# First chunk behind a full-width norm taken as two summands, and made whole last

## The reference

```python
for layer in range(DEPTH):                                  # DEPTH = 2
    h = rms_norm(r, norm_mix_pre[layer])
    proj = h @ w_in[layer]                                  # latents first, then q, k, v, gates
    ...                                                     # MLA and differential attention, gates
    mix = (sigmoid(g_a) * out_a + sigmoid(g_b) * out_b) @ w_out[layer]
    r = r + rms_norm(mix, norm_mix_post[layer])
    h = rms_norm(r, norm_ffn_pre[layer])
    gu = h @ w_gate_up[layer]
    ff = (silu(gu[..., :D_FF]) * gu[..., D_FF:]) @ w_down[layer]
    r = r + rms_norm(ff, norm_ffn_post[layer])
```

## Time and profile before

| What | Value |
| --- | --- |
| Median of 3 runs | 794.01 us |
| Profiled execution | 794.08 us |
| Its span | 792.3 us |
| PE busy | 785.0 us, 99% of the span |
| DVE busy | 572.3 us, 72% |
| ACT busy | 451.7 us, 57% |
| POOL busy | 138.6 us, 17% |
| TensorE clock granted | 0.999 of full, mean |
| HBM traffic | 169 GB/s over the span |

### The profile page before, as it was taken

How to read it: one execution, slowest core, us unless ns; L and a number is a source line. 1 busy time by engine, 2 the same in 40 slices (tenths; PEclk the granted TensorE clock), 3 DMA queues, 4 the chain that set the end, 5 groups by cost and what they waited for, 6 DMA issues and landing times.

```text
span 792.3 us, 16792 instructions
## 1 busy us (share of the span) xinstructions
PE 785.0 (99%) x6268; PEld 762.2 (96%) x6268; DVE 572.3 (72%) x996; ACT 451.7 (57%) x766; POOL 138.6 (17%) x150
## 2 busy tenths in 40 slices
PE   9999999999999999999999999999999999999997
PEld 9999899999999999999999999999999999999885
DVE  6899787696787666766668987967866977676432
ACT  6657665675475454455557467656755755454331
POOL 0312000233321111101123302001433211111000
PEclk9999999999999999999999999999999999999999
DMA  9767433355166565355654674334552776667971
GB/s 334 255 225 241 131 109 107 107 187 160 55 206 218 161 176 172 115 166 170 198 173 134 192 241 153 107 108 132 187 167 73 227 215 178 195 175 193 276 135 54
DMA packets 55531, 134.87 MB, mean 170 GB/s; under 512 B 20896, under 2 KB 21536, under 8 KB 55344
## 3 DMA queue, kind: packets, MB, share of 16 engines
q1 hardware_dynamic: 38608, 131.43, 52.9%
q10 hardware_dynamic: 16864, 2.62, 2.0%
HBM read 131.93 MB, written 2.10 MB: 169 GB/s over the span
## 4 chain that ended last, share of the span: by engine, by line
PE 97%; DVE 1%; ACT 1%; issue 0%; DVEq 0%
PE bank L1330 24%; PE bank L1332 24%; PE bank L1331 24%; PE bank L1364 4%; PE bank L1748 3%; PE bank L1749 3%; PE bank L1747 3%; PE bank L1355 2%; PE bank L1602 2%; PE bank L1574 2%; PE bank L1621 1%; PE bank L1449 1%; PE bank L1423 1%; PE bank L1576 1%; PE bank L1380 1%; PE bank L1391 1%
## 5 line engine op out<-in xcount | busy, mean ns | idle before, releaser
L883 DVE TENSOR_TENSOR w_lo<-w_raw,w_hi 128x1024 fp32r<-128x1024 f32 x246 | 330.9, 1348 | 37.4 <-ACT w_hi L438 34.5
L1330 PE MATMUL bank<-h_hi,w_hi 128*128 128x272 f32 (+1 forms) x1200 | 346.0, 288 | 0.0
L1332 PE MATMUL bank<-h_hi,w_lo 128*128 128x272 f32 (+1 forms) x1200 | 342.8, 286 | 0.0
L1331 PE MATMUL bank<-h_lo,w_hi 128*128 128x272 f32 (+1 forms) x1200 | 341.9, 285 | 0.0
L438 ACT ACTIVATE w_hi<-w_raw 128x1024 fp32r<-128x1024 f32 x246 | 258.5, 1054 | 122.1 <-PE bank L1332 57.0
L1330 PEld LDWEIGHTS bank<-h_hi,w_hi 128*128 128x128 f32 x1200 | 226.2, 188 | 0.7
L1332 PEld LDWEIGHTS bank<-h_hi,w_lo 128*128 128x128 f32 x1200 | 226.2, 188 | 0.0
L1331 PEld LDWEIGHTS bank<-h_lo,w_hi 128*128 128x128 f32 x1200 | 226.0, 188 | 0.0
L848 POOL TENSOR_TENSOR pbuf<-sbuf,ubuf 128x272 f32<-128x272 f32 (+1 forms) x44 | 38.5, 874 | 205.6 <-DVE ubuf L1260 204.0
L779 POOL TENSOR_TENSOR acc<-acc,sq 128x272 f32<-128x272 f32 (+1 forms) x45 | 47.3, 1052 | 137.2 <-ACT sq L451 137.0
L1260 DVE TENSOR_TENSOR ubuf<-bank,rstd_h 128x272 f32<-128x272 f32 (+1 forms) x44 | 18.9, 430 | 44.9 <-PE bank L1332 44.9
(11 more groups left out here) (238 smaller groups left out, 1229.2 us busy)
## 6 DMA issues: line engine op xcount, KB each, us to landing
w_raw<-weights SPq DMA_DIRECT2D x216, 512.0 KB, 3.9
w_raw<-weights SPq DMA_DIRECT2D x16, 384.0 KB, 3.2
w_raw<-weights SPq DMA_DIRECT2D x16, 320.0 KB, 2.9
w_first<-first_weights SPq DMA_DIRECT2D x2, 512.0 KB, 7.5
x_tok<-x_rows SPq DMA_DIRECT2D x1, 1024.0 KB, 11.0
turn<-y ACTq DMA_DIRECT2D x4, 256.0 KB, 7.1
r_tok<-turn ACTq DMA_DIRECT2D x8, 128.0 KB, 6.3
out_tokens<-o_tok SPq DMA_DIRECT2D x4, 256.0 KB, 2.0
```

What stands on the lines that cost most here:

```text
L883: dve.tensor_tensor(w_lo[:, n % RING, :], w_raw[:, n % RAW, :], w_hi[:, n % RING, :].bitcast(f32), ALU.subtract).then_inc(lo_ready, 1)
L1330: pe.matmul(dst, wh, hi, start=first, stop=False)
L1331: pe.matmul(dst, wh, lo, start=False, stop=False)
L1332: return pe.matmul(dst, wl, hi, start=False, stop=last)
```

## The change

Chunk 0 of the stream behind a post-norm is `old + new`: the old residual, known early, and the normed part's product. Both times the gain are split into high and low parts of their own. ACT makes `old_hi` behind the sixth output tile, DVE `old_lo` behind the seventh. The PE multiplies the first four tiles' weights of chunk 0 with the old part inside `post_norm`: two tiles ahead of the transposes in place of 10 dummy matmuls, two tiles behind them, with 8 dummies in place of 28. Behind the transposes DVE makes `new` first, ACT rounds it to `new_hi`, and the first tiles take it as their chunk 0. DVE and ACT then make chunks 1 to 7, and last the whole chunk 0 (`CHUNK_ORDER`). The fifth tile takes the chunks in that order; it has the norm sums ahead of its fifth chunk, and the spread (FFN only) ahead of its last. Its last chunk waits for all low parts. In `first_tiles` the bank waits of the boundaries move into `old_part`, one for each tile.

```diff
+CHUNK_ORDER = [1, 2, 3, 4, 5, 6, 7, 0]
...
+            def old_high(b):
+                t0 = boundary_from(b)
+                act.activation(old_hi[:, t0:], r[:, 0, t0:], ACT.Copy, scale=first_gain(b)).then_inc(old_hi_ready, 1)
...
-                for c in range(KC):
-                    act.wait_ge(r_ready, KC * (b - 1) + c + 1)
+                act.wait_ge(new_ready, b)
+                act.activation(new_hi[:, t0:], new[:, t0:], ACT.Copy, scale=first_gain(b)).then_inc(new_hi_ready, 1)
+                for c in CHUNK_ORDER:
+                    if c == 0:
+                        act.wait_ge(r_first_ready, b)
+                    else:
+                        act.wait_ge(r_ready, (KC - 1) * (b - 1) + c)
+                    high(c)
+                    square(K, CHUNK_ORDER.index(c), r[:, c, t0:], t0)
...
                     square_tile(K0 + POST_MIX, TL("out") + m, m)
+                    if m == 5:
+                        old_high(2 * l + 1)
...
+                dve.scalar_tensor_tensor(out=new[:, t0:], in0=y[:, 0, t0:], scalar=gain[:, lp, gp:gp + 1],
+                                         in1=ps[7][:, 64 + t0:64 + TOK], op0=ALU.mult, op1=ALU.mult).then_inc(new_ready, 1)
...
-                product(0)
-                add(0)
                 product(1)
                 add(1)
-                for c in range(2, KC):
+                product(2)
+                new_low()
+                add(2)
+                for c in range(3, KC):
                     product(c)
                     lo_part(b, c - 2, *nxt(b), t0)
                     add(c)
                 lo_part(b, KC - 2, *nxt(b), t0)
+                dve.wait_ge(new_ready, b)
+                dve.tensor_tensor(r[:, 0, t0:], r[:, 0, t0:], new[:, t0:], ALU.add).then_inc(r_first_ready, 1)
                 lo_part(b, KC - 1, *nxt(b), t0)
+                lo_part(b, 0, *nxt(b), t0)
...
                     to_y(K0 + POST_MIX, TL("out") + m, m)
+                    if m == 6:
+                        old_low(2 * l + 1)
...
+            def fifth_tile(b, t, n, src, t0, inside):
+                bank_free(t)
+                for at, k in enumerate(CHUNK_ORDER):
+                    if at in inside:
+                        inside[at]()
+                    if k == 0:
+                        pe.wait_ge(h_lo, KC * (b + 1))
+                    mm = block(t, n, k * P, P, *src[k], t0, at == 0, at == KC - 1)
+                mm.then_inc(pe_done, 1)
...
+            def old_part(b, tiles):
+                pe.wait_ge(old_lo_ready, b)
+                slot_ready(tiles[-1][1])
+                for t, n, _, t0 in tiles:
+                    bank_free(t)
+                    dst = ps[bank_of(t)][:, t0:TOK]
+                    pe.matmul(dst, w_hi[:, n % RING, 0:P], old_hi[:, t0:], start=True, stop=False)
+                    pe.matmul(dst, w_lo[:, n % RING, 0:P], old_hi[:, t0:], start=False, stop=False)
+                    pe.matmul(dst, w_hi[:, n % RING, 0:P], old_lo[:, t0:], start=False, stop=False)
...
-            def post_norm(K):
+            def post_norm(K, b, tiles):
                 norm_sums(K, 7, t0)
-                keep_clock(10)
+                old_part(b, tiles[:2])
                 norm_spread(K, 7, t0)
-                keep_clock(28)
+                old_part(b, tiles[2:])
+                keep_clock(8)
...
+                slot_ready(g0 + 4)
+                fifth_tile(2 * l + 1, gt + 4, g0 + 4, late, t0, {4: lambda: norm_sums(K0 + PRE_FFN, 7, t0), 7: lambda: norm_spread(K0 + PRE_FFN, 7, t0)})
```

More of the change, by code:

```diff
@@ L254, in build_trunk @@
             ("ubuf", [P, 2, TOK], f32), ("sbuf", [P, 2, TOK], f32), ("pbuf", [P, 2, TOK], f32)])
+        (old_hi, old_lo, new_hi, new_lo, new), _end = place(att0 + 4 * 2 * FC * TOK, [
+            ("old_hi", [P, TOK], f32r), ("old_lo", [P, TOK], f32r), ("new_hi", [P, TOK], f32r), ("new_lo", [P, TOK], f32r), ("new", [P, TOK], f32)])
+        assert _end <= _
         (gain_bc, r_tok), _ = place(_, [("gain_bc", [P, D_MODEL], f32), ("r_tok", [P, 2, D_MODEL], f32)])
@@ L363, in boundary_from, with nxt, first_gain, made_before @@
             return N_META if b >= 2 * DEPTH - 1 else 0
+        def nxt(b):
+            return (G_FFNPRE, b // 2) if b % 2 else (G_MIXPRE, b // 2)
+        def first_gain(b):
+            g, l = nxt(b)
+            return gain[:, l, g:g + 1]
+        def made_before(b, c):
+            return KC * b + (CHUNK_ORDER.index(c) if b else c)
         @block.sync
@@ L1341, in tile, with first_tiles, part, part_ready @@
                 mm.then_inc(pe_done, 1)
-            def first_tiles(tiles, ready):
-                if tiles[0][1]:
+            def old_part(b, tiles):
[7 more added lines that the diff above has]
+                    pe.matmul(dst, w_hi[:, n % RING, 0:P], old_lo[:, t0:], start=False, stop=False)
+            def first_tiles(tiles, ready, b=0):
+                if not b:
                     slot_ready(tiles[-1][1])
-                bank_free(max((t for t, *_ in tiles), key=lambda t: -1 if plan.before[t] is None else plan.before[t]))
+                    bank_free(max((t for t, *_ in tiles), key=lambda t: -1 if plan.before[t] is None else plan.before[t]))
                 hi_sem, lo_sem, base = ready
+                def part(q, k, src, t0):
+                    if b and k == 0:
+                        return (new_hi, new_lo)[q][:, t0:]
+                    return src[k][q]
+                def part_ready(q, k):
+                    if b and k == 0:
+                        pe.wait_ge((new_hi_ready, new_lo_ready)[q], b)
+                    else:
+                        pe.wait_ge((hi_sem, lo_sem)[q], (made_before(b, k) if b else base + k) + 1)
                 def low(k):
-                    pe.wait_ge(lo_sem, base + k + 1)
+                    part_ready(1, k)
                     for t, n, src, t0 in tiles:
-                        mm = pe.matmul(ps[bank_of(t)][:, t0:TOK], w_hi[:, n % RING, k * P:(k + 1) * P], src[k][1],
+                        mm = pe.matmul(ps[bank_of(t)][:, t0:TOK], w_hi[:, n % RING, k * P:(k + 1) * P], part(1, k, src, t0),
                                        start=False, stop=k == KC - 1)
@@ L1360, in first_tiles @@
                 for k in range(KC):
-                    pe.wait_ge(hi_sem, base + k + 1)
+                    part_ready(0, k)
                     for t, n, src, t0 in tiles:
                         for q, w in enumerate((w_hi, w_lo)):
-                            pe.matmul(ps[bank_of(t)][:, t0:TOK], w[:, n % RING, k * P:(k + 1) * P], src[k][0],
-                                      start=k == 0 and q == 0, stop=False)
+                            pe.matmul(ps[bank_of(t)][:, t0:TOK], w[:, n % RING, k * P:(k + 1) * P], part(0, k, src, t0),
+                                      start=not b and k == 0 and q == 0, stop=False)
                     if k:
@@ L1460, in norm_spread, with h_from, latent_tiles @@
                 spread(K, bank, t0)
+            def h_from(a):
+                return [(hh[:, k, a:], hl[:, k, a:]) for k in range(KC)]
+            def latent_tiles(l):
+                start = [T0(l) if q < QC else 0 for q in range(BANKS)]
+                return [(plan.tile[l, "lat", q], plan.slot[l, "lat", q], h_from(a), a) for q, a in enumerate(start)]
             pe.wait_ge(warm_ready, 1)
@@ L1467, in _ @@
                 TL = lambda name, i=0: plan.tile[l, name, i]
-                full = [(hh[:, k, :], hl[:, k, :]) for k in range(KC)]
-                late = [(hh[:, k, t0:], hl[:, k, t0:]) for k in range(KC)]
+                full, late = h_from(0), h_from(t0)
                 if l == 0:
@@ L1474, in _ @@
                 else:
-                    first_tiles([(TL("lat") + q, S("lat") + q, *((late, t0) if q < QC else (full, 0))) for q in range(BANKS)],
-                                (h_hi, h_lo, KC * 2 * l))
+                    first_tiles(latent_tiles(l), (h_hi, h_lo, KC * 2 * l), 2 * l)
                 slot_ready(S("lat") + 4)
-                tile(TL("lat") + 4, S("lat") + 4, 0, P, full, 0, inside={0: lambda: norm_sums(K0 + PRE_MIX, 7, 0)} if l else None)
+                if l == 0:
+                    tile(TL("lat") + 4, S("lat") + 4, 0, P, full, 0)
+                else:
+                    fifth_tile(2 * l, TL("lat") + 4, S("lat") + 4, full, 0, {4: lambda: norm_sums(K0 + PRE_MIX, 7, 0)})
                 slot_ready(S("lat") + 5)
@@ L1709, in _ @@
                     tile(TL("out") + m, S("out") + m, 0, P, late, t0)
[L1710 removed]
                 g0, gt = S("gu"), TL("gu")
[L1713 to L1714 removed]
+                tiles = [(gt + q, g0 + q, late, t0) for q in range(BANKS)]
+                post_norm(K0 + POST_MIX, 2 * l + 1, tiles)
+                first_tiles(tiles, (h_hi, h_lo, KC * (2 * l + 1)), 2 * l + 1)
+                slot_ready(g0 + 4)
+                fifth_tile(2 * l + 1, gt + 4, g0 + 4, late, t0, {4: lambda: norm_sums(K0 + PRE_FFN, 7, t0), 7: lambda: norm_spread(K0 + PRE_FFN, 7, t0)})
```

(2 more changed lines are left out.)

27 lines of the change are left out of this document (20 added, 7 removed).

## The result

The changed kernel takes 795.48 us (median of 16 runs, 794.85 to 796.29) against 794.07 for the kernel before (16 runs): ratio 1.0016, 95% interval 1.0010 to 1.0023. It is 1.4 us slower, and the interval does not hold 1. The forecast was 795.0, a loss of 1.0, in a range of 793.1 to 796.0. The profiled execution took 795.39 for a span of 793.6, so the span grew by 1.3. The chain's line of shares now reads 96% PE and has 1% of "issue".

A forecast was written before the change was run, and what follows sets the result against it. The PE, carrying 97% of the chain, was taken as the bound, with short stretches behind post-norms where it only passes time. Terms −1.26 + 0.93 + 1.29 = +0.96 took the median from 794.01 to 795.0, range 793.1 to 796.0.

The forecast's parts named there:

- The step that decided the sign: Fifth tile's later sums and spread empty the third gate/up tile late; the seventh, sharing its bank, stalls: +0.93 and +1.29.
- Link removed, +0.05 push, gain 0.42: Behind each post-norm: dropping DVE's add saves 0.47 to 0.48, transposes end about 0.05 later; three boundaries give −1.26.
- Twelve more matmuls covered: At each boundary the wait for the normed part covers the 12 added matmuls; uncovered they would cost 1.5.
- the PE fed afterwards: In the first tiles DVE gives a chunk every 1.29, the PE takes one every 1.5: no wait.
- old part's making free: At the sixth and seventh output tiles, ACT's rounding (0.52) and DVE's low part (0.5) cost nothing; uncovered, 0.1 each.
- Seventh tile behind the first boundary, stall 0.93: After layer 0's mixer: emptying 0.72 later, at 225.47, while the PE would be there at 224.74; +0.93.
- Second boundary, nothing lost: Behind layer 0's FFN: sums move but ACT reads them over six microseconds later, no gate/up tiles follow; nothing lost.
- Seventh tile behind the third boundary, stall 1.29: Behind layer 1's mixer: Silu, split and emptying 0.87 later, from a PE 0.42 earlier; +1.29, or 1.05 by spread alone.
- No drain behind the table load: Before Silu: the skill's drain of about 1.38 left out as the trace shows none; with it, an estimated 797.7.
- The kept gain: Rival: the seventh tile finds its bank free, so the boundary gain of 1.26 stays, giving 792.75; chance 0.13.
- A push: Rival: old part's six matmuls pay their waits ahead of the spread, 0.45 worse per boundary, giving 796.3; chance 0.10.
- The clock: Rival: fewer dummies let the PE clock fall over one boundary's first tiles, 12 more, giving 807; chance 0.03.

The follow-up runs named there:

- e8: e1 without the eight dummy matmuls behind the old part: 792.65 us against 793.98 for the kernel before, ratio 0.9983.
- e1: Changed kernel with the fifth tile's norm sums back ahead of its first chunk and the spread ahead of its fifth: 792.49 us against 793.95 for the kernel before.
- e6: e1 with all twelve old-part matmuls behind the transposes, ten dummies ahead of them and the eight behind left out: 792.75 us against 793.98 for the kernel before.
- e4: Changed kernel with POOL's first product of layer 1 held until DVE has emptied the third gate/up tile: 794.97 us against 793.95 for the kernel before.
- e10: Changed kernel with DVE emptying the third gate/up tile before the weight split ahead of it, both layers: 792.73 us against 794.07 for the kernel before.
- e5: Changed kernel with sums ahead of the fifth tile's first chunk and spread ahead of its fourth: 793.00 us against 793.98 for the kernel before.
- e9: e5 with POOL's first product of layer 1 held until the third gate/up tile is emptied: 792.56 us against 794.07 for the kernel before.
- e7: e1 with ten dummy matmuls added between the old part's first half and the transposes: 794.17 us against 793.98 for the kernel before, ratio 1.0004.
- e3: Kernel before with only the later places, sums ahead of the fifth tile's fifth chunk, spread ahead of its last: 797.01 us against 793.95, ratio 1.0035.
- e2: Changed kernel with only the sums back ahead of the fifth tile's first chunk, spread still ahead of its last: 794.68 us against 793.95 for the kernel before.

## Why the prediction was right

The step that decided the sign stood: a tile's bank behind the fifth tile, read off, which the edit never mentions. One term of the sum was too small. Point by point:

- *Link removed, +0.05 push, gain 0.42.* Measured 0.49 at the first boundary. The transposes start 0.13 later, inside the 0.15 that the prediction allowed, and the push on DVE's product was 0.08; but the PE starts 0.05 behind the rounding's end (205.17) and not 0.14. That is not because the dummies keep it busy: in `e8` it has been idle for 0.4 and starts 0.06 behind. The waits for banks and slots that stood at this place before are elsewhere now; whether they made the difference was not tested. `e1` has −0.43 to −0.50 in each stretch.
- *Twelve more matmuls covered, the PE fed afterwards, old part's making free.* Held: the first tiles run without a gap, and `e1` and `e6` agree.
- *Seventh tile behind the first boundary, stall 0.93.* Measured 1.01 less the pitch, 0.88, and 0.08 of a restart (second matmul at 225.54, 0.21 behind the first). The prediction's own terms, 225.47 + 0.11 + 0.07 against 224.74, give 0.91, not 0.93. The stretch grew by 0.50, net of the gain, against a forecast of 0.51; that it fits to 0.01 is luck, with stretches that scatter by up to 0.2.
- *Second boundary, nothing lost.* The stretch gave 0.33; the other kernels with the same boundary gave 0.36 to 0.54. The missing 0.1 to 0.2 shows at the next pre-norm: its transposes start 0.23 behind the matmul ahead of them, where 0.12 is the pitch, and the matmul behind them comes at 431.39, where it would be at 431.24 in step with `e1`. ACT's root came at 430.31 behind a weight split that had waited 0.88 for its DMA (0.55 in `e4`). `e4` and `e10`, the same program there, gave 0.52 and 0.54, so it is probably the run; nothing here tests it further.
- *Seventh tile behind the third boundary, stall 1.29.* This is the mis-sized term: 1.91 less 0.12 = 1.79. Silu came within 0.1 of its forecast place (0.75 later against 0.87, of which 0.07 is that run's shift); 0.55 was added by POOL's product, which the sum had at nothing. `e4`, `e5` and `e9` show it from both sides: without it the stall is 1.23. The three stretches were forecast at +0.51, −0.42 and +0.87, +0.96 in all, and measured at +0.50, −0.33 and +1.37; nearly all of the difference is this term.
- *No drain behind the table load.* In the changed kernel's timeline the load at 613.90 takes 1.28 and Silu starts at 615.20, 0.02 behind its end. The Trainium skill (ScalarE: Activation LUTs, What ACT_TABLE_LOAD costs) has a drain of about 1.38 there; here the measurement decides against it.
- *The rivals.* The kept gain is real, 792.5 in `e1`, but not for this edit. A push is paid one for one (`e7`), but this edit's is small. The clock did not move: in the three boundary stretches of every kernel here the granted clock is 1.00, and behind the idle stretches of `e8` the matmuls are 0.12 apart. The price that the prediction put on it, 0.109 a dummy at the start of the kernel, is not a reading of that column, though: the window 1.00 to 5.65 of the kernel before has a granted clock of 1.00 as well, so what makes those dummies slow the profile does not say.

## What to carry to other kernels

When a step that many wait for (a norm's spread, a table load) is moved by a microsecond on an engine that is always busy, follow it to the first buffer that is reused and write down how much room that reuse has; 0.41 and 0 were all there was here. Then ask which instructions of other engines now start in another order on the way. An emptying that frees a bank goes ahead of bulk work that only fills a ring several slots deep. A gain on a chain at the front and a loss on a chain behind it can come from one edit: test them apart before judging either.

## What the hardware did that was not expected

POOL's additions and products of SBUF tensors and DVE's weight split cost one another time by who starts first. At the seventh tile, POOL ahead by 0.05 to 0.08: the split takes 1.75 to 1.78 (`e3`, `e5`, the changed kernel). DVE ahead by 0.16: the split takes 1.22 or 1.23 and POOL's product 1.65 to 1.67, where it takes 0.74 when it is first (kernel before, `e1`, `e2`; in `e4` and `e9` POOL meets the next split instead, in the same way). The trace of the kernel before had it already, 7 us ahead of the split in question:

```profile
608.20 0.94 POOL L779 TENSOR_TENSOR acc<-acc,sq 128x256 f32<-128x256 f32 x1 [0.34 <-ACT sq L451]
...
608.46 1.76 DVE L883 TENSOR_TENSOR w_lo<-w_raw,w_hi 128x1024 fp32r<-128x1024 f32 x1
```

The sizes follow one pattern in that trace. Around the three boundaries (196 to 236, 400 to 436 and 590 to 632) there are 11 splits that overlap a POOL instruction that had started first, by 0.10 to 1.32; all end 1.08 or 1.09 behind POOL's end. In 8 cases the split started first, by 0.16 to 0.87, and POOL ends 0.59 to 0.64 behind it. The row at 616.60 fits: POOL's product ends at 617.29 and the split at 618.38. The Trainium skill (SBUF — State Buffer, SBUF: two separate sides) says that a DVE instruction with two SBUF inputs and a GpSimd (POOL) instruction that reads SBUF share one pair of ports, that the first to start holds it for its whole instruction and that the other is blocked. The traces agree; the blocked split needs 1.08 from there and not its full 1.22.

So a shift of some 0.2 us in who is first was worth 0.4 to 0.6 us of the PE's time, and made an earlier spread (`e5`) slower than a later one (`e1`). A forecast that shifts either engine should work out both starts, and put the blocked one's end at the first one's end plus 1.08 for this split, or plus 0.6 for POOL's instruction.
